# Identity products on TensorE at fifteen of its waits

## What is computed

```python
# first block, x is [1, 256, 1024]
h = rmsnorm(x, norm_mix_g[0])
ya = rwkv7_group(h, ...)         # 8 heads of 64, scan over time, done in chunks of 64
yb = gdn_group(h @ w_in, ...)    # 4 heads of 128, gated delta rule in chunks of 64
x = x + concat([ya, yb]) @ even_w_out
x = x + relu(rmsnorm(x) @ mlp_w1[0])**2 @ mlp_w2[0]      # then a gated embedding of p[0]
x = x + chunk_band_attention(rmsnorm(x), ...) @ attn_w_out
x = x + relu(rmsnorm(x) @ mlp_w1[1])**2 @ mlp_w2[1]      # then a gated embedding of p[1]
# second block: two layers, modulated by mod = silu(c) @ w_ada + b_ada
x_l = x_l + g1 * even_mixer(modulate(x_l), modulate(x_c))   # neighbourhood and differential attention
x_l = x_l + g2 * conv_ffn(modulate(x_l)); x_c likewise
x_l = x_l + g1 * odd_mixer(modulate(x_l), modulate(x_c))    # grouped attention and hyena
x_l = x_l + g2 * conv_ffn(modulate(x_l))
```

## Time and profile before

| what | value |
|---|---|
| median of 3 runs | 2194.58 us (2194.24 to 2197.38) |
| profiled execution | 2192.41 us |
| its span, first to last instruction | 2190.6 us |
| PE busy | 2081.6 us, 95% of the span |
| DVE busy | 1164.5 us, 53% |
| ACT busy | 375.0 us, 17% |
| chain that ended last, by engine | PE 85%, DVE 10%, DMA 2%, ACT 2% |

### The profile page before, as it was taken

How to read it: one execution, slowest core, us unless ns; L and a number is a source line. 1 busy time by engine, 2 the same in 40 slices (tenths; PEclk the granted TensorE clock), 3 DMA queues, 4 the chain that set the end, 5 groups by cost and what they waited for, 6 DMA issues and landing times.

```text
span 2190.6 us, 24522 instructions
## 1 busy us (share of the span) xinstructions
PE 2081.6 (95%) x10662; PEld 1468.8 (67%) x10662; DVE 1164.5 (53%) x1656; ACT 375.0 (17%) x752; POOL 10.8 (0%) x22
## 2 busy tenths in 40 slices
PE   6999898899989989999999989999999999989998
PEld 5886665696448559844784454788884456549973
DVE  2642676374521346653544582555545765546775
ACT  2413110100021320001112461111110012221110
POOL 0000000000000000000000000000000000000000
PEclk9999998999999999999999999999999999999999
DMA  4324686344444324453223101222224453123443
GB/s 162 147 82 170 239 348 268 130 160 187 153 169 158 116 92 155 161 204 128 92 88 120 39 1 39 77 77 77 77 88 173 171 206 135 39 77 116 159 150 115
DMA packets 22459, 292.66 MB, mean 134 GB/s; under 512 B 2720, under 2 KB 2848, under 8 KB 4304
## 3 DMA queue, kind: packets, MB, share of 16 engines
q1 hardware_dynamic: 20576, 280.66, 34.0%
q0 software_dynamic: 1776, 10.43, 1.3%
HBM read 290.03 MB, written 1.05 MB: 133 GB/s over the span
## 4 chain that ended last, share of the span: by engine, by line
PE 85%; DVE 10%; DMA 2%; ACT 2%; issue 1%; DVEq 0%; ACTq 0%
PE bank L325 83%; DMA ring<-in_W 2%; DVE small L851 1%; PE bank L630 1%; DVE arena L872 1%; DVE arena L592 1%; PE bank L783 0%; DVE HT L674 0%; DVE arena L1017 0%; DVE arena L641 0%; DVE arena L865 0%; DVE arena L550 0%; DVE HT L679 0%; DVE arena L846 0%; ACT arena L817 0%
## 5 line engine op out<-in xcount | busy, mean ns | idle before, releaser
L325 PE MATMUL bank<-arena 128*128 128x128 f32 (+9 forms) x3856 | 683.2, 352 | 20.0 <-ACT arena L817 3.6
L325 PEld LDWEIGHTS bank<-arena 128*128 128x128 f32 (+3 forms) x3856 | 477.4, 185 | 207.5 <-issue 155.0
L325 PE MATMUL bank<-HT,ring 128*128 128x256 f32 (+1 forms) x2416 | 460.7, 350 | 12.7 <-DVE HT L679 8.8
L325 PEld LDWEIGHTS bank<-HT,ring 128*128 128x128 f32 x2416 | 401.0, 193 | 66.2 <-DVE HT L679 9.3
L325 PE MATMUL bank<-ring,arena 128*128 128x512 f32 x690 | 302.4, 593 | 3.6 <-DMA ring<-in_W 3.6
L325 PEld LDWEIGHTS bank<-ring,arena 128*128 128x128 f32 x690 | 130.0, 190 | 166.4 <-issue 165.9
L325 PE MATMUL bank<-ring,HT 128*128 128x512 f32 (+2 forms) x512 | 197.8, 545 | 7.9 <-ACT arena L639 3.1
L325 PE MATMUL bank<-arena,ring 128*128 128x128 f32 (+2 forms) x1046 | 172.4, 322 | 0.4 <-issue 0.4
L325 PEld LDWEIGHTS bank<-ring,HT 128*128 128x128 f32 x512 | 91.4, 195 | 111.0 <-issue 101.5
L325 PEld LDWEIGHTS bank<-arena,ring 128*128 128x128 f32 (+1 forms) x1046 | 152.9, 191 | 13.5 <-issue 1.8
L639 ACT ACTIVATE arena<-bank 128x512 f32<-128x512 f32 (+2 forms) x127 | 69.3, 570 | 514.5 <-PE bank L325 486.2
(11 more groups left out here) (303 smaller groups left out, 1523.8 us busy)
## 6 DMA issues: line engine op xcount, KB each, us to landing
ring<-in_W SPq DMA_DIRECT2D x125, 2048.0 KB, 7.7
ring<-in_W SPq DMA_DIRECT2D x6, 1536.0 KB, 9.3
ring<-in_W SPq DMA_DIRECT2D x4, 1024.0 KB, 9.7
arena<-in_rel POOLq DMA_DIRECT2D x1, 2048.0 KB, 9.8
arena<-in_rpb POOLq DMA_DIRECT2D x1, 2048.0 KB, 9.5
arena<-in_dft POOLq DMA_DIRECT2D x2, 640.0 KB, 6.8
KC<-in_const SPq DMA_DIRECT2D x1, 1057.5 KB, 9.5
X<-in_x SPq DMA_DIRECT2D x1, 1024.0 KB, 4.9
```

The source lines that it names most:

```text
L325: return nc.tensor.matmul(out_, lhsT, rhs, start=start, stop=stop, skip_group_check=True)
```

## The change

A helper `pe_fill(n, b)` issues `n` products of the 128x128 identity by itself into a bank, by default the next one in turn without taking it. It signals nobody, and nothing reads what it writes. It is called ahead of TensorE's waits; `pe_norm` gets a pair of numbers, one call ahead of its first wait and one ahead of its last. A call with 0 issues no product. The rest of the program is as it was. The sites with products:

```diff
+        def pe_fill(n, b=None):
+            b = state["bank"] % 8 if b is None else b
+            ps = open_bank("fill", b)
+            for _ in range(n):
+                mm(ps[:, 0:P], K("ident"), K("ident"), True, True)
+            state["last"][b] = None
-        def pe_norm(label, tiles, xn):
+        def pe_norm(label, tiles, xn, fill=(0, 0)):
+            pe_fill(fill[0])
             for t in tiles:
                 pe.wait_ge(vector_done, at(f"{label} xn {t}"))
                 for h in range(2):
                     pe_turn(f"{label} turned {t}.{h}", ...)
+            pe_fill(fill[1])
             pe.wait_ge(vector_done, at(f"{label} ready {tiles[-1]}"))
         def pe_bgate(t):
             if t == 0:
+                pe_fill(6)
                 state["block"] = weight("bgate")...
                 pe_turn(f"vt{t}", [VF[:, g, t * P:(t + 1) * P] for g in range(4)])
+            pe_fill(6, banks["vt0"])
             pe_inverse_first("rwkv", 4, XT1)
             pe_chunk_out(0)
+            pe_fill(10, banks["ada6"])
             pe_ada(8)
                 if c > 0:
+                    if c == 2:
+                        pe_fill(12, banks["ob0"])
                     pe_bchunk_in(c)
                     pe_ada(20 + c)
                 pe_bchunk_out(c)
+            pe_fill(6)
             pe_mod(1)
                     pe_turn(f"ymix turned {t}.{h}", ...)
+                if h == 0:
+                    pe_fill(8)
                 for t in range(2):
                     pe.wait_ge(scalar_done, at(f"read ymix turned {t}.{h}"))
-            pe_norm(f"ffn{i}", [0, 1], M["xn"])
+            pe_norm(f"ffn{i}", [0, 1], M["xn"], (7, 2 if i else 6))
-            pe_norm("mix1", [0, 1], XN3)
+            pe_norm("mix1", [0, 1], XN3, (17, 2))
-            w = weight_of(pe_norm, f"cffn{i}", [0, 1], F["xn"], f"cup{i}.0")
+            w = weight_of(pe_norm, f"cffn{i}", [0, 1], F["xn"], f"cup{i}.0", (9, 16) if i else (0, 16))
+            def win_tokens():
+                pe_fill(11)
+                pe.wait_ge(vector_done, at("win tokens"))
+            pe_fill(10)
             pe_gate(0, 0, 0)
```

More of the change, by code:

```diff
@@ L2297, in pe_turn_tile, with weight_of @@
                 pe_turn(f"{label} turned {t}.{h}", [xn[:, t % 2, (4 * h + i) * P:(4 * h + i + 1) * P] for i in range(4)])
-        def weight_of(norm, label, tiles, xn, name):
-            norm(label, tiles, xn)
+        def weight_of(norm, label, tiles, xn, name, fill):
+            norm(label, tiles, xn, fill)
             return weight(name).rearrange("p (k c) -> p k c", k=KT)
@@ L2600, in pe_even @@
                 pe_seven_rows(f"win {p}", w_pairs[p], w_groups, EWS, EWT, lambda k, t: HT[:, k, (1 - t) * SEQ:(2 - t) * SEQ], SEQ,
-                              seq=None if p else w_seq, between={(0, 4): lambda: sums_of("qd", "kd")} if p else {(1, 1): x_turn, (1, 2): lambda: pe.wait_ge(vector_done, at("win tokens"))})
+                              seq=None if p else w_seq, between={(0, 4): lambda: sums_of("qd", "kd")} if p else {(1, 1): x_turn, (1, 2): win_tokens})
+            pe_fill(10)
             pe_gate(0, 0, 0)
```

## The result

| | before | after |
|---|---|---|
| median of the runs | 2194.41 us (2193.99 to 2197.38, 4 runs) | 2173.74 us (2171.52 to 2176.19, 4 runs) |
| profiled execution | 2192.41 us | 2171.52 us |
| its span | 2190.6 us | 2169.7 us |
| PE busy | 2081.6 us x10662 | 2092.1 us x10964 |

The ratio is 0.9903, with a 95% interval from 0.9886 to 0.9920: the change makes the kernel 1.0% faster. The title speaks of fifteen waits; the calls with products are seventeen.

What follows compares the result with a forecast made beforehand. TensorE bounds the kernel, busy 95% of the span, with waits that bring its clock down. Nine terms sum to 21.0 us, taking the profiled 2192.4 to 2171.4 us; with 2.2 us distance to the median, 2173.6 us, range 2166 to 2189.

Steps and rivals of the forecast that it cites:

- The coupling: At TensorE's gaps: a gap costs its own length, then up to half of the 3.4 to 10.2 us that follow.
- all five: Gains at the low stretches at 374.5, 654.4, 808.0, 1374.6 and 1971.9: 3.0, 2.6, 0.2, 2.6 and 2.6 us.
- 3.6 for 340 to 371: Low stretch at 357.4: half its busy time, 4.6 us, less 1.0 for a DVE step, gives 3.6 us.
- 1.8 at 265.2: Low stretch at 265.2: half its busy time is 2.9 us, but DVE's work limits the gain to 1.8 us.
- The terms at 98.0 and 197.0: Low stretches after `vt` and at `pe_bgate`: half their busy time taken whole as gain, 1.7 and 2.9 us.
- rival 4: At the fills: clock already low or falling, a product costs 0.47 us, kernel slower at 2224 us; chance 0.06.
- c == 2: Twelve products (2.6 us) ahead of `pe_bchunk_in(2)` at 351.2, not in a gap: cost nothing, 0.8 us spare.
- The signs to look for: Profile after: 302 more matmuls, gaps under 1.0 us at the calls, mean clock near 0.997, gain behind the gaps.
- 1: Fills ahead of transposes: transposes do not hold the clock, stretches at 654.4, 808.0, 1971.9 stay, 2179 us; chance 0.12.
- 2: At some calls the fill is not enough, or sparse products count less; half the sum missed, 2184 us; chance 0.12.
- 3: At all calls: products are hidden but the clock does as before, 2194.6 us; chance 0.05.
- 5: Stretches without a call (343.75, 756.8, 1910.5) vanish as well: 5.1 us more, 2168.5 us; chance 0.05.

Runs made afterwards that it cites:

- e10_after: The changed kernel as it is, run again on another chip beside the kernel before: 2174.7 us, ratio to before 0.9912.
- e1_none: The changed kernel with zero products at all seventeen calls, banks still opened early: 2189.5 us, ratio to before 0.9996.
- e12_norms: The changed kernel with products only at the calls of `pe_norm`, 82 of the 151: 2185.7 us, ratio to before 0.9973.
- e4_narrow: The changed kernel with the same number of products, each of 8 columns of the identity instead of 128: 2194.0 us, ratio to before 1.0015.
- e11_probe: The changed kernel plus 30 products ahead of the up projection's third pair, 8 columns in mlp0, 128 in mlp1: 2192.9 us, one execution.
- e3_turns: The changed kernel with each product replaced by two transposes of the identity: 2174.4 us, ratio to before 0.9929.

## Why the prediction was right, point by point

- **The time.** Forecast 2173.6 us, measured 2173.7; for the profiled execution 2171.4 and 2171.5. Such agreement is partly luck, as the table of terms shows: the start gave 2.1 us that no call touches, at the call after `vt` 1.2 us were lost instead of 1.7 gained, and one more stretch went than was counted. The two profiled executions were also both good ones of their kernel: after had 17 us of low time where the same kernel in e10_after had 27, and before had none behind the gaps of 2.81 and 2.65 us, where three other executions without full-width products there had some.
- **The coupling** of gap and low stretch: shown by e1_none, and by e12_norms, where the calls that are left keep their own places at full clock and the others fall. e4_narrow narrows it: what has to stand in the gap is full-width work.
- **The terms.** From 371 on, all five are right within 0.1 us, and the sixth, 3.6 for 340 to 371, is right with the 1.7 of the stretch at 343.75, which had been counted as staying (5.3 together). The cut of one term for DVE (1.8 at 265.2) was too deep: 2.7 came. In these places halving the busy time of a low row was a good price.
- **The terms at 98.0 and 197.0 failed.** The step that failed is to take a stretch as gone because the fill fits the gap ahead of it. At 98.0 the term had 1.7 us and the place lost 1.2. The fill itself cost nothing (the work behind the gap comes 2.1 us earlier than before, as it did ahead of it), but a stretch of 6.8 us stands there now instead of 3.4, as in e1_none and e12_norms, which have no products there. So the gap that the call fills does not decide it. At 197.0 the call halved the stretch instead of removing it, 1.8 us of 2.9. At both places narrow work stands near: 16 matmuls of 2 columns and 32 of 64 columns at 99.1 to 105.7 of after, and 32 of 8 columns just before `pe_bgate`. After the change the clock fell while PE was busy, as e11_probe shows that it can; that the narrow work is the cause at these two places is argued and not shown. The fill at 195.2 ran mostly at half clock:

```profile
191.70 3.64 PE L325 MATMUL bank<-ring,HT 128*128 128x8 f32 x32
195.20 2.58 PE L325 MATMUL bank<-KC 128*128 128x128 f32 x12
197.57 3.02 PE L325 MATMUL bank<-ring,HT 128*128 128x512 f32 x5
```

  Six products in 2.58 us in a gap of 1.69 us: rival 4 came true at this one place, and cost 0.5 us there before the shorter low stretch gave back 2.3.
- **The price of a product**: 0.22 forecast, 0.233 measured (3.96 us for 17, drain included); it was covered nearly everywhere.
- **The bank waits** at zero, and c == 2: right. The twelve products at 344.40 take 2.95 us and `pe_bchunk_out(2)` still waits 0.77 us, where 0.8 us were forecast to be spare.
- **The signs to look for.** The mean clock is 0.995, not 0.997, since the stretches at 103 and 196 are there. Two gaps are over 1.0 us (1.10 at 646.08 and its like in mlp1), because the transposes ahead of them are faster now and DVE is not. The last sign was that the executions in the median may have had more low stretches than the profiled one of before. On the first chip that isn't known; on the other three chips before has a mean clock of 0.980 over 55 executions, against 0.983 in the profiled one, so it is likely, and the 2.2 us kept as a distance may stand for part of it.
- **The rivals.** 1 fell with e3_turns. 2 held at two places, and sparse operands, which it named, are not the reason (the identity holds the clock elsewhere). 3 fell. 5 held in one of its three stretches in this execution; in the execution of e10_after a short one is back at 338.6, and another of 3.4 us at 355.7, behind a place with products, so these come and go.

What stays open: why the clock falls after a given gap or narrow block in one execution and not in the next, and why the stretch after `vt` does not follow its gap. Only one execution of each kernel was profiled, but the mean granted clock is known of every execution beside the variants. Over the 55 executions of the kernel before on the three later chips it ranges from 0.976 to 0.984 and goes with the time (correlation -0.73): the two at 0.976 took 2196.4 us on average, the four at 0.983 took 2187.4. So a good part of the 13 us of spread of the kernel before goes with the clock. Which stretches it is in each execution is not known.

## What to carry to other kernels

Where TensorE bounds a kernel, price a wait of it at its own length plus half of the busy time that the trace shows at the low clock behind it (look at more than one execution, since the same gap may or may not be followed by such a stretch), and look for these stretches by cutting the span at the granted clock, not by the mean. Full-width products or transposes of a constant (here the identity), put ahead of a wait into a bank that is free, kept the clock in most places, at no cost where they ended before the wait did; leave some room, since twice as many gave the whole gain back. Take each call out once and look at the trace: the one after `vt` gave nothing. Look also at runs of narrow products: they count as busy, cost what wide ones cost here, and can lose the clock for the work behind them.

## What was not expected of the hardware

- Products of 8 columns take as long as those of 128 (0.114 us per matmul, 32 in 3.64 us), look as busy, and after 3.7 us of them in otherwise dense work the clock fell for 10.2 us. With 128 columns it did not. At another place 3.64 us of them were followed by a fall in some executions and not in others.
- Transposes in float32 hold the full clock for over 7 us by themselves (e3_turns, 1.00 from 639.7 to 649.9).
- TensorE's first work runs as slowly as at the low clock (16 transposes in 3.65 us at 17.8, against 8 in 1.09 later), though the clock column of the profile has 1.00 there. How long this lasts varies: the 32 products of 256 columns behind took 9.1 us in one execution and 7.2 in another, 1.9 us for two kernels that are the same up to there.
- The low stretches of all fourteen profiled executions came in three lengths, leaving out the end: 3.4, 6.8 and 10.2 us.
